# Sharing the residual update of three norms between two engines, and moving four other pieces of work

## The chip, the cores and the metric

One core of a Trainium2 chip runs the whole program. The time is the device time of one execution in microseconds (us), lower is better. Profiled executions add a span (first to last instruction) and a trace.

## What is computed

Two transformer layers over 512 tokens of width 1024 (with 256 context tokens beside them in layer 0), then a third block with windowed attention and a mixture of experts. Cut to what matters here:

```python
for i in range(2):                      # layer i; the context rows are dropped after layer 0
    hx = rmsnorm(x, g_pre_mix[i]) * (1 + sc1) + sh1        # "premix" norm
    px = hx @ w_in[i]
    attn = attention(rope(q), rope(k), v)                  # 8 heads, keys of x and of ctx
    four = fft2(px[..., F0:H0]).real @ w_fourier[i]
    hy   = x0 * longconv(x1 * v, filter)                   # hyena
    x = x + ga1 * rmsnorm(concat(attn, four, hy) @ w_out[i], g_post_mix[i])   # "postmix", then "preffn"
    x = x + ga2 * rmsnorm(conv_ffn(rmsnorm(x)...), g_post_ffn[i])             # "postffn"
# third block: attention, router, experts; each token goes to the two best of 16 experts
```

The modulation vectors (`sc1`, `sh1`, `ga1`, ...) are a product of the condition with a large matrix, whose slabs are streamed in between the other weights.

## The kernel before, in words

Activations lie transposed: 8 blocks of 128 channels (`x[:, k, :]`) by 768 tokens (layer 0, `T`) or 512 (`TX`). Each product is done in three passes of split operands (a high part and a remainder), so every weight slab of 128x1024 is loaded by a DMA of SyncE, copied to `whi` by ScalarE and its remainder `wlo` is made by GpSimd (L585). A ring of three slots holds the raw slabs; SyncE loads the next one when a slot is free (L506 to L512). The order on each engine is the order of the code; semaphores tie the engines.

**Norm to norm.** After the output product, `post_norm` (L1966) gates the 8 blocks of `y` on VectorE (two instructions a block at 768 tokens, one at 512). GpSimd adds block k to `x` when it is gated (L591). ScalarE squares it (`norm_stats`, L1407) into one of two buffers, TensorE sums the squares (L718), and when the eighth is summed the inverse root mean square goes back over ScalarE, VectorE and TensorE to the scaling of the next norm. This happens four times: layer 0 postmix (768 tokens), layer 0 postffn (768), layer 1 postmix (512) and layer 1 postffn, which the change leaves as it is.

**Fourier and first attention steps.** TensorE makes `fab` tiles (L909), waits for all of them and for all five rotated heads (`k_roped`), and runs for f = 0, 1 the second Fourier product (L941, segment 0 of 512 tokens and in layer 0 segment 1 of 256), each followed by the scores of two attention steps (L928, `scores(0)` and `scores(2)`). Then comes the output product (L954), then six transposes of the values (L961), ScalarE's `values_hi` and VectorE's `values_lo`, and only then the first transposes of probabilities (L971). From there attention is a loop of equal steps.

**Hyena.** `hy_pair(p)` multiplies two slabs of the modulation matrix (L755, eight instructions); they lie in the ring's slots, and the loads of the next pair are issued when a pair is used. `mod_turn` (L763) transposes the result of two pairs. Pairs 0 and 1 and the turn stand before the first transform product, pair 2 behind the second product of f = 0, pair 3 inside f = 1, pair 4 inside f = 3. The filter product (L1033) waits for the table `hd5`, the input product is L1045, the inverse L1066.

**Experts.** GpSimd issues four scatters of token rows to `slot_rows` (L614), waits until they have landed, issues seven loads `xs` (L617, L619), and only then makes the remainders `mlo` of 21 of the 168 expert slabs (L623), VectorE those of the others (L2568). TensorE's product of the second expert (`gate_up(1)`, slab 1) needs the first of them, its third expert (`gate_up(2)`) begins with `turn_block(1, 0)`, which waits for all the loads `xs` (L1313). Raw expert slabs stand in 8 slots; SyncE loads slab n when the remainder of slab n - 8 is made, so slab 13 waits for GpSimd's first remainder (slab 5).

Of the kernel before, what the change touches and what calls it, by code (L numbers as in the profile page):

```python
# [29 lines left out]
P = 128  # L30
D = 1024
KT = D // P
# [116 lines left out]
def program(nc, dram, out):  # L149
# [187 lines left out]

    def sum_nth(key):

        return 0 if key == norms[0] else 1 + post_nth(key)  # L340
# [231 lines left out]
    def _(pool):  # L572
# [38 lines left out]
        pool.wait_ge(sem("slots_clear"), 16)  # L611
        pool.wait_ge(sem("routed"), 5)
        for tt in range(TX // P):
            pool.indirect_dma_start(slots_d, bass.IndirectOffsetOnAxis(slot_i[:, tt:tt + 1], 0), xrow[:, tt, :], None)\  # L614
                .then_inc(sem("rows_placed"), 16)
        pool.wait_ge(sem("rows_placed"), 16 * (TX // P))
# [3 lines left out]
        for u, j in M_POOL:  # L620
            n = M_AT[(u, j)]
            pool.wait_ge(ring_hi, n + 1)
            pool.tensor_tensor(mlo2[:, n % MS, :], mraw2[:, n % MR, :], mhi2[:, n % MS, :].bitcast(F32),  # L623
                               ALU.subtract).then_inc(pool_lo, 1)
# [8 lines left out]
    def _(pe):  # L633
# [174 lines left out]
        for L in range(DEPTH):  # L808
# [122 lines left out]

            pe.wait_ge(sem("fab_ready"), T // P * L + ntt)
            pe.wait_ge(sem("k_roped"), 5 * L + 5)
            for f in range(2):
# [24 lines left out]
            pe.wait_ge(sem("qk_lo"), 5 * L + 5)  # L959
            for tt in range(6):  # L960
                m = pe.transpose(ps[:, 4 + tt // 4, (tt % 4) * P:(tt % 4) * P + P], pxq[:, PXV, tt * P:tt * P + P],  # L961
                                 ident[:, :])
            m.then_inc(sem("vt_done"), 1)
# [51 lines left out]
            hy_pair(1)  # L1015
            mod_turn(HY_G[L], 3)
            two = len(hsegs[L]) == 2
            for s, c0, nt_ in hsegs[L]:
# [9 lines left out]
                for f in range(nt_):  # L1028
# [20 lines left out]
                    if s == 0 and f == 0:  # L1049
                        hy_pair(2)  # L1050
# [330 lines left out]
    def _(act):  # L1381
# [19 lines left out]
        def norm_stats(key, src, width, ready=None, before=0):  # L1401
            for k in range(KT):
                if ready is not None:
                    act.wait_ge(ready, before + k + 1)
                if k >= 2:
                    act.wait_ge(sem("sq_used"), (KT + 1) * sq_nth(key) + k - 1)
                act.activation(nsq[:, k % 2, 0:width], src[:, k, 0:width], ACT.Square)\  # L1407
                   .then_inc(sem("sq_ready"), 1)
# [73 lines left out]
        for L in range(DEPTH):  # L1482
# [3 lines left out]
            else:  # L1486
                norm_stats((L, "premix"), x, T, sem("x_ready"), KT * post_nth((L - 1, "postffn")))
# [7 lines left out]
            if L == 0:  # L1495
                act.dma_start(fl2[:, :, :, :], dram["four256"]).then_inc(sem("ftab_in", L), 16)
                act.dma_start(slots_d, dram["slot_rows"]).then_inc(sem("slots_clear"), 16)
# [94 lines left out]

            def scaled_act(i):
# [6 lines left out]
            for f in range(2):  # L1600
# [18 lines left out]

            def values_hi():  # L1620
                act.wait_ge(sem("vt_done"), L + 1)
                for g in range(2):
                    h = slice(64 * g, 64 * g + 64)
                    m = act.activation(vth[:, g, :, h], psf[:, 2048:2048 + 768].rearrange("p (t n) -> p t n", t=6)[:, :, h],
                                       ACT.Copy)
                m.then_inc(sem("pt_hi"), 1)
# [12 lines left out]
            values_hi()  # L1639
# [32 lines left out]
            for s, c0, nt_ in hsegs[L]:  # L1672
                w = nt_ * P
                K = (L, s)
                for f in range(nt_):
# [6 lines left out]
                    if s == 0 and f == 1:  # L1682
# [26 lines left out]
            norm_stats((L, "preffn"), x, W, sem("x_ready"), KT * post_nth((L, "postmix")))  # L1709
# [45 lines left out]
        unnormed((2, "premix"), TX, sem("x_ready"), KT * post_nth((1, "postffn")),  # L1755
# [164 lines left out]
    def _(dve):  # L1920
# [45 lines left out]
        def post_norm(key, L, gate, width, low=None):  # L1966

            inverse_rms(key, width)
            for k in range(KT if low is None else KT + 3):
# [5 lines left out]
                if low is not None and k >= 3:  # L1975
                    low(k - 3)
            dve.drain()
# [50 lines left out]
        for L in range(DEPTH):  # L2028
# [116 lines left out]
            for c in range(2):  # L2145
                bv = V0 + V_HYB + c
                dve.tensor_scalar(hub[:, c, 0:W], pxh[:, 2 + c, 0:W], vec[:, bv:bv + 1], None, ALU.mult)
            if L == 0:
# [28 lines left out]
            minimum(2)  # L2177
            minimum(3)
# [12 lines left out]
            def values_lo():  # L2191
                dve.wait_ge(sem("pt_hi"), (HALVES0 + 1) * L + 1)
                for g in range(2):
                    h, other = slice(64 * g, 64 * g + 64), slice(64 - 64 * g, 128 - 64 * g)
                    dve.memset(vth[:, g, :, other].bitcast(F32), 0.0)
                    dve.memset(vtl[:, g, :, other].bitcast(F32), 0.0)
                    m = dve.tensor_tensor(vtl[:, g, :, h], psf[:, 2048:2048 + 768].rearrange("p (t n) -> p t n", t=6)[:, :, h],
                                          vth[:, g, :, h].bitcast(F32), ALU.subtract)
                m.then_inc(sem("pt_lo"), 1)

# [10 lines left out]
            values_lo()  # L2211
# [219 lines left out]
        dve.wait_ge(sem("router_in"), 64)  # L2431
# [391 lines left out]
```

## Time and profile before

| | us |
|---|---|
| median of 3 runs (2543.62 to 2550.24) | 2543.91 |
| profiled execution | 2553.14 |
| its span | 2551.3 |
| TensorE busy in it | 2343.3 (92%) |
| VectorE, ScalarE, GpSimd busy | 1285.1, 1099.0, 652.1 |
| mean granted TensorE clock (of 2.4 GHz) | 0.954 |

PE is TensorE (PEld its weight loads), DVE VectorE, ACT ScalarE, POOL GpSimd, SP SyncE; a letter q behind a name is its queue or sequencer. In a timeline row the columns are start, duration, engine, line, operation, what is written <- what is read, shape and count; in brackets stands how long the engine had been idle and who released it. A row of several instructions gives their busy time together.

### The profile page before, as it was taken

The numbers are of one execution on the slowest core, as the hardware profiler recorded it, in microseconds if no ns is written. First come the engines' busy times: TensorE is split into PE (matmuls) and PEld (weight loads), VectorE is DVE, ScalarE is ACT, GpSimd is POOL, SyncE is SP. The second block draws the span as 40 slices with busy tenths as digits, with TensorE's granted clock in tenths as the row PEclk, the third lists the DMA queues.
The fourth block names the chain that finished last, engine by engine and source line by source line (L and its number), as shares of the span: only waits on it lengthen the run. The fifth ranks groups of instructions, "written<-read, shape, count | busy, mean of one in ns | idle before, by whom it ended". The sixth has DMA issues, their size and how long they took to land.

```text
span 2551.3 us, 32346 instructions
## 1 busy us (share of the span) xinstructions
PE 2343.3 (92%) x12442; PEld 1869.8 (73%) x12442; DVE 1285.1 (50%) x2040; ACT 1099.0 (43%) x1687; POOL 652.1 (26%) x295
## 2 busy tenths in 40 slices
PE   4998979979999999988989888999999999979997
PEld 2875856858888788866657566888876877767776
DVE  3565942153431344235667214534524269449998
ACT  3423840353332333225357035434423268447776
POOL 1220000242222222342300034444444410222223
PEclk8999999979999999988989998999999999989999
DMA  6421032113222232112400441233332322249997
GB/s 240 174 96 34 1 118 97 58 36 114 92 66 67 83 118 73 58 50 95 140 1 32 151 148 59 96 95 98 99 97 69 98 69 59 111 152 366 346 350 262
DMA packets 81466, 291.27 MB, mean 114 GB/s; under 512 B 10761, under 2 KB 13226, under 8 KB 80364
## 3 DMA queue, kind: packets, MB, share of 16 engines
q1 hardware_dynamic: 74192, 257.68, 30.0%
q10 hardware_dynamic: 4252, 20.58, 2.2%
q0 software_dynamic: 2880, 11.06, 1.1%
q8 instruction: 96, 1.57, 0.2%
q14 instruction: 46, 0.38, 0.0%
HBM read 283.50 MB, written 9.48 MB: 115 GB/s over the span
## 4 chain that ended last, share of the span: by engine, by line
PE 77%; DVE 11%; ACT 3%; DMA 2%; POOL 2%; issue 2%; DVEq 1%; SPq 0%; POOLq 0%; ACTq 0%
PE ps L647 37%; PE ps L694 12%; DVE mlo L2568 5%; PE ps L670 4%; PE ps L985 3%; PE ps L971 2%; PE ps L1347 2%; PE ps L755 2%; PE ps L1207 2%; PE ps L928 2%; POOL x L591 1%; PE ps L941 1%; PE ps L1045 1%; PE ps L1066 1%; DMA wraw<-in_w_all 1%
## 5 line engine op out<-in xcount | busy, mean ns | idle before, releaser
L585 POOL TENSOR_TENSOR wlo<-wraw,whi 128x1024 fp32r<-128x1024 f32 x208 | 502.1, 2415 | 1386.1 <-ACT whi L1388 738.9
L647 PE MATMUL ps<-hhi,whi 128*128 128x512 f32 x1624 | 591.8, 364 | 3.0 <-DVE hlo L2265 2.0
L647 PE MATMUL ps<-hlo,whi 128*128 128x512 f32 x1624 | 583.3, 359 | 0.0
L647 PE MATMUL ps<-hhi,wlo 128*128 128x512 f32 x1624 | 580.7, 358 | 0.0
L647 PEld LDWEIGHTS ps<-hhi,whi 128*128 128x128 f32 x1624 | 306.2, 189 | 83.3 <-issue 31.2
L647 PEld LDWEIGHTS ps<-hhi,wlo 128*128 128x128 f32 x1624 | 305.3, 188 | 47.9
L647 PEld LDWEIGHTS ps<-hlo,whi 128*128 128x128 f32 x1624 | 306.2, 189 | 45.3 <-issue 1.0
L1982 DVE SCALAR_TENSOR_TENSOR up<-ps,cconv,up 128x511 f32<-128x511 f32 (+1 forms) x132 | 83.1, 658 | 294.9 <-ACT up L1725 292.3
L2568 DVE TENSOR_TENSOR mlo<-mraw,mhi 128x1024 fp32r<-128x1024 f32 x147 | 203.8, 1415 | 9.7 <-ACT mhi L1851 9.2
L1395 ACT ACTIVATE whi<-wraw 128x1024 fp32r<-128x1024 f32 x132 | 138.9, 1052 | 152.6 <-PE ps L694 120.3
L1725 ACT ACTIVATE up<-ps,cconv 128x768 f32<-128x768 f32 (+1 forms) x88 | 77.8, 884 | 257.7 <-PE ps L647 257.2
L694 PE MATMUL ps<-alo,whi 128*128 128x512 f32 (+1 forms) x528 | 188.0, 356 | 0.0
L694 PE MATMUL ps<-ahi,whi 128*128 128x512 f32 (+1 forms) x528 | 187.4, 355 | 0.0
L694 PE MATMUL ps<-ahi,wlo 128*128 128x512 f32 (+1 forms) x528 | 186.6, 353 | 0.0
L1851 ACT ACTIVATE mhi<-mraw 128x1024 fp32r<-128x1024 f32 x168 | 167.4, 1050 | 5.7 <-DMA mraw<-in_w_moe 5.3
L2314 DVE TENSOR_TENSOR y<-y,ps 128x768 f32<-128x768 f32 (+1 forms) x32 | 26.2, 820 | 227.6 <-PE ps L694 227.6
L1388 ACT ACTIVATE whi<-wraw 128x1024 fp32r<-128x1024 f32 x76 | 80.2, 1057 | 111.5 <-PE ps L647 86.8
L694 PEld LDWEIGHTS ps<-ahi,whi 128*128 128x128 f32 x528 | 99.6, 189 | 15.0
L694 PEld LDWEIGHTS ps<-ahi,wlo 128*128 128x128 f32 x528 | 99.2, 188 | 14.8
L694 PEld LDWEIGHTS ps<-alo,whi 128*128 128x128 f32 x528 | 99.5, 188 | 13.8
L623 POOL TENSOR_TENSOR mlo<-mraw,mhi 128x1024 fp32r<-128x1024 f32 x21 | 62.8, 2990 | 177.0 <-ACT mhi L1851 177.0
L670 PE MATMUL ps<-hhi,whi 128*128 128x512 f32 (+1 forms) x168 | 68.3, 406 | 31.8 <-DVE hlo L1960 23.1
(360 smaller groups left out, 4210.7 us busy)
## 6 DMA issues: line engine op xcount, KB each, us to landing
wraw<-in_w_all SPq DMA_DIRECT2D x288, 512.0 KB, 3.6
mraw<-in_w_moe SPq DMA_DIRECT2D x168, 512.0 KB, 5.7
mraw_b<-in_w_mod SPq DMA_DIRECT2D x10, 512.0 KB, 15.4
fl<-in_four ACTq DMA_DIRECT2D x2, 2048.0 KB, 8.2
hi<-in_hyi ACTq DMA_DIRECT2D x2, 2048.0 KB, 8.7
slot_rows<-in_slot_rows ACTq DMA_DIRECT2D x1, 3612.0 KB, 20.9
xs<-slot_rows POOLq DMA_DIRECT2D x7, 516.0 KB, 6.9
mraw_a<-in_w_mod SPq DMA_DIRECT2D x6, 512.0 KB, 10.5
```

Of the source, the lines that this page charges most:

```text
L585: pool.tensor_tensor(wlo[:, slot, :], wraw[:, AT_W[n] % RING, :], whi[:, slot, :].bitcast(F32), ALU.subtract).then_inc(lo_split, 1)
L623: pool.tensor_tensor(mlo2[:, n % MS, :], mraw2[:, n % MR, :], mhi2[:, n % MS, :].bitcast(F32), ALU.subtract).then_inc(pool_lo, 1)
L647: m = pe.matmul(ps[:, bank + b, 0:w], a, r[:, c0:c0 + w], start=k == 0 and q == 0, stop=k == KT - 1 and q == 2)
L670: m = pe.matmul(ps[:, bank + b, 0:w], a, r[:, c0:c0 + w], start=k == 0 and q == 0, stop=k == KT - 1 and q == 2)
L694: m = pe.matmul(ps[:, bank + b, 0:w], a, r[:, c0:c0 + w], start=k == 0 and z == 0, stop=k == PAIRS - 1 and z == 2)
L985: m = pe.matmul(ps[:, 6 + ht % 2, c0:c0 + HALF], u[:, g, kts[c], :], w[:, unit % 2, c, g * HALF:g * HALF + HALF], start=g == 0 and c == 0 ...
L1388: act.activation(whi[:, n % RING, :], wraw[:, AT_W[n] % RING, :], ACT.Copy).then_inc(hi_split, 1)
L1395: act.activation(whi[:, n % RING, :], wraw[:, AT_W[n] % RING, :], ACT.Copy).then_inc(hi_split, 1)
L1725: act.activation(up[:, p % 2, z, 0:W], psf[:, b * 512:b * 512 + W], ACT.Identity, bias=cconv[:, s, 3:4], scale=cconv[:, s, 1:2]).then_inc( ...
L1851: act.activation(mhi2[:, m % MS, :], mraw2[:, n % MR, :], ACT.Copy).then_inc(ring_hi, 1)
L1982: dve.scalar_tensor_tensor(dst[:, c0 + 1:c0 + w], ps[:, bank + b, 0:w - 1], w0, dst[:, c0 + 1:c0 + w], ALU.mult, ALU.add)
L2568: dve.tensor_tensor(mlo2[:, m % MS, :], mraw2[:, n % MR, :], mhi2[:, m % MS, :].bitcast(F32), ALU.subtract).then_inc(ring_lo, 1)
```

## The change

Five edits. (1) In three of the four post norms GpSimd adds blocks 0 to 4 and VectorE blocks 5 to 7, with a semaphore of its own; ScalarE squares in the order 0, 1, 2, 3, 5, 4, 6, 7. (2) The transposes of the values stand behind the first Fourier segment and use PSUM banks 0 and 1, the wait for the rotated heads stands behind that segment, `values_hi` and `values_lo` follow at once; `scores(0)` stands behind segment 0 of f = 1 and `scores(2)` behind the output product, and ScalarE's and VectorE's parts follow that order. (3) In hyena one pair stands between the two products of each of the four f, and the turns behind the second product of f = 0 and 2. (4) GpSimd makes its first `mlo` before it waits for the scatters. (5) The clearing of `slot_rows` counts on `router_in`.

```diff
+    def pool_adds(key):
+        return KT if key == (DEPTH - 1, "postffn") else 5
+    def added(key, k):
+        n = post_nth(key)
+        return (sem("x_ready"), 5 * n + k + 1) if k < pool_adds(key) else (sem("x_late"), 3 * n + k - 4)
...
-                for k in range(KT):
+                for k in range(pool_adds(key)):
                     pool.wait_ge(sem("y_gated"), KT * post_nth(key) + k + 1)
...
                 if key[1] == "postmix":
+                    pool.wait_ge(sem("x_late"), 3 * post_nth(key) + 3)
                     pool.drain()
...
+        mlo(*list(M_POOL)[0])
         pool.wait_ge(sem("rows_placed"), 16 * (TX // P))
...
-        for u, j in M_POOL:
...
+        for u, j in list(M_POOL)[1:]:
+            mlo(u, j)
...
             pe.wait_ge(sem("fab_ready"), T // P * L + ntt)
-            pe.wait_ge(sem("k_roped"), 5 * L + 5)
...
-                if f == 0:
-                    pe.wait_ge(sem("qk_lo"), 5 * L + 5)
-                scores(2 * f)
+                    if s == 0 and f == 0:
+                        pe.wait_ge(sem("k_roped"), 5 * L + 5)
+                        turned_values()
+                    if s == 0 and f == 1:
+                        pe.wait_ge(sem("qk_lo"), 5 * L + 5)
+                        pe.wait_ge(sem("pt_lo"), (HALVES0 + 1) * L + 1)
+                        scores(0)
...
+            scores(2)
...
-            hy_pair(1)
-            mod_turn(HY_G[L], 3)
...
-                    if s == 0 and f == 1:
-                        hy_pair(3)
-                    if s == 0 and f == 2:
-                        mod_turn(HY_G[L] + 1, 3)
-                    if s == 0 and f == 3:
-                        hy_pair(4)
+                    if s == 0:
+                        hy_pair(1 + f)
...
-                    if s == 0 and f == 0:
-                        hy_pair(2)
+                    if s == 0 and f in (0, 2):
+                        mod_turn(HY_G[L] + f // 2, 3)
...
+            for k, b in enumerate((0, 1, 2, 3, 5, 4, 6, 7)):
+                act.wait_ge(*added(post, b))
...
-                exponentials(2 * f)
-                exponentials(2 * f + 1)
-                if f == 0:
-                    scaled_act(1)
+                    if s == 0 and f == 0:
+                        values_hi()
+            exponentials(0)
+            exponentials(1)
+            scaled_act(1)
...
+            exponentials(2)
+            exponentials(3)
...
-                    if s == 0 and f == 1:
+                    if s == 0 and f == 2:
                         rows(HY_G[L] + 1, 3)
...
+            def add(k):
+                dve.tensor_tensor(x[:, k, 0:width], x[:, k, 0:width], y[:, k, 0:width], ALU.add)\
+                   .then_inc(sem("x_late"), 1)
...
+                if pool_adds(key) < KT and k >= 6:
+                    dve.drain()
+                    add(k - 1)
+            if pool_adds(key) < KT:
+                add(KT - 1)
```

## Rows read from the trace of the kernel before

**Rows 1.** Page, part 4: shares of the chain that ended last.

```profile
PE 77%; DVE 11%; ACT 3%; DMA 2%; POOL 2%; issue 2%; DVEq 1%; SPq 0%; POOLq 0%; ACTq 0%
```

**Rows 2.** Timeline of layer 0's postmix to preffn norm, 768 tokens.

```profile
512.65 8.49 DVE L1972 SCALAR_TENSOR_TENSOR y<-y,mv,ps 128x512 f32<-128x512 f32 x16 [2.32 <-PE ps L747]
513.87 14.22 POOL L591 TENSOR_TENSOR x<-x,y 128x768 f32<-128x768 f32 x8 [1.34 <-DVE y L1972]
...
528.12 0.84 ACT L1407 ACTIVATE nsq<-x 128x768 f32<-128x768 f32 x1 [0.93 <-POOL x L591]
...
529.02 1.08 PE L718 MATMUL ps<-nsq,ones 128*32 128x256 f32 x8 [0.69 <-ACT nsq L1407]
```

**Rows 3.** Timeline of layer 1's postmix to preffn norm, 512 tokens.

```profile
1525.49 9.86 POOL L591 TENSOR_TENSOR x<-x,y 128x512 f32<-128x512 f32 x8
...
1536.07 0.66 PE L718 MATMUL ps<-nsq,ones 128*32 128x128 f32 x8 [0.57 <-ACT nsq L1407]
```

**Rows 4.** Line 2302: operation, count, duration in ns (min/median/max), starts, forms.

```profile
L2302 DVE TENSOR_TENSOR alo<-sil,ahi x44: 691/825/961, 569.5 to 1853.0; 128x768 fp32r<-128x768 f32 x22, 128x512 fp32r<-128x512 f32 x22
```

**Rows 5.** Timelines of VectorE and of GpSimd, early in the experts.

```profile
2305.65 3.40 DVE L2568 TENSOR_TENSOR mlo<-mraw,mhi 128x1024 fp32r<-128x1024 f32 x2 [0.76 <-ACT mhi L1851]
...
2303.96 2.88 POOL L623 TENSOR_TENSOR mlo<-mraw,mhi 128x1024 fp32r<-128x1024 f32 x1 [12.01 <-ACT mhi L1851]
```

**Rows 6.** Timeline of layer 0, Fourier to the first attention loop step.

```profile
214.29 0.60 ACT L1570 ACTIVATE fab<-ps 128x512 f32<-128x512 f32 x1 [0.30 <-PE ps L909]
...
216.23 10.53 PE L941 MATMUL ps<-fl,fab 128*128 128x512 f32 x24 [1.98 <-DVE pxq L2131]
...
227.94 8.86 PE L941 MATMUL ps<-fl,fab 128*128 128x512 f32 x24
...
237.97 5.43 PE L954 MATMUL ps<-fy,wfo 128*128 128x512 f32 x16
...
240.84 0.86 ACT L1617 ACTIVATE hhi<-ps 128x512 fp32r<-128x512 f32 x2
...
249.75 0.49 ACT L1635 ACTIVATE pth<-ps 128x384 fp32r<-128x384 f32 x1 [3.62 <-PE ps L971]
```

**Rows 7.** Timeline of the same stretch in layer 1.

```profile
1282.55 10.02 PE L941 MATMUL ps<-fl,fab 128*128 128x512 f32 x16 [4.48 <-DVE pxq L2131]
...
1293.74 7.13 PE L941 MATMUL ps<-fl,fab 128*128 128x512 f32 x16
...
1312.58 0.49 ACT L1635 ACTIVATE pth<-ps 128x384 fp32r<-128x384 f32 x1 [3.62 <-PE ps L971]
```

**Rows 8.** One window: busy time by engine, then PEclk, DMA share, GB/s.

```profile
218.00:220.00 2.00, 2.00 (x3) 0.69 (x3) 2.00 (x4) 0.63 (x2) 0.00 (x0) 0.50 0.00 0
```

**Rows 9.** DMA issues (KB, us to landing), then timeline, of hyena in layer 0.

```profile
hd<-in_hyf ACTq DMA_DIRECT2D x1, 512.0 KB, 4.7
...
367.07 5.19 PE L1033 MATMUL ps<-hpm,hd 128*128 128x256 f32 x16
...
382.60 1.06 PE L755 MATMUL ps<-wraw,cs 128*32 128x512 f32 x8 [2.24 <-DMA wraw<-in_w_all]
383.59 5.41 PE L1045 MATMUL ps<-hut,hd 128*128 128x256 f32 x16
...
392.73 3.62 PE L1045 MATMUL ps<-hut,hd 128*128 128x256 f32 x16
```

**Rows 10.** Hyena in layer 1: chain (start, duration, what), then timeline.

```profile
1397.43 9.62 DMA hd<-in_hyf
...
1423.25 1.07 PE L755 MATMUL ps<-wraw,cs 128*32 128x512 f32 x8 [2.27 <-DMA wraw<-in_w_all]
```

**Rows 11.** Experts: a wait; GpSimd's DMA queue (packets, MB, share), 2283-2296, 2276-2280.

```profile
PE ps L1347 <- POOL mlo L623: 4.7, 1, 4.7
...
q0 software_dynamic: 990, 3.65, 74.0%
...
q0 software_dynamic: 204, 0.78, 47.2%
```

More of the change, by code:

```diff
@@ L609, in _ @@
                     m.then_inc(sem("osum_ready"), 1)
-        pool.wait_ge(sem("slots_clear"), 16)
+        pool.wait_ge(sem("router_in"), 16)
         pool.wait_ge(sem("routed"), 5)
@@ L615, in _, with mlo @@
                 .then_inc(sem("rows_placed"), 16)
+        def mlo(u, j):
+            n = M_AT[(u, j)]
+            pool.wait_ge(ring_hi, n + 1)
+            pool.tensor_tensor(mlo2[:, n % MS, :], mraw2[:, n % MR, :], mhi2[:, n % MS, :].bitcast(F32),
+                               ALU.subtract).then_inc(pool_lo, 1)
+        mlo(*list(M_POOL)[0])
         pool.wait_ge(sem("rows_placed"), 16 * (TX // P))
@@ L619, in _ @@
             pool.dma_start(xs[:, b, :], slots_d[b * P:b * P + P, :]).then_inc(sem("blocks_in"), 16)
-        for u, j in M_POOL:
[L621 to L624, printed above, removed]
+        for u, j in list(M_POOL)[1:]:
+            mlo(u, j)
         for b in range(BLOCKS):
@@ L930, in scores, with turned_values @@
                 m.then_inc(sem("s_ready"), 2)
+            def turned_values():
+                for tt in range(6):
+                    m = pe.transpose(ps[:, tt // 4, (tt % 4) * P:(tt % 4) * P + P], pxq[:, PXV, tt * P:tt * P + P],
+                                     ident[:, :])
+                m.then_inc(sem("vt_done"), 1)
             pe.wait_ge(sem("fab_ready"), T // P * L + ntt)
-            pe.wait_ge(sem("k_roped"), 5 * L + 5)
             for f in range(2):
@@ L955, in _ @@
                     m.then_inc(sem("fst3"), 1)
+            scores(2)
             pe.wait_ge(sem("k_roped"), 5 * L + 5)
             pe.wait_ge(sem("four_out"), 4 * L + 2 * len(fseg))
[L959 to L963, printed above, removed]
             def transposed(i):
@@ L1399, in rms, with norm_stats @@
                .then_inc(sem("std_ready"), 1)
[L1401 to L1404, printed above, removed]
+        def norm_stats(key, width, post):
+            for k, b in enumerate((0, 1, 2, 3, 5, 4, 6, 7)):
+                act.wait_ge(*added(post, b))
                 if k >= 2:
                     act.wait_ge(sem("sq_used"), (KT + 1) * sq_nth(key) + k - 1)
-                act.activation(nsq[:, k % 2, 0:width], src[:, k, 0:width], ACT.Square)\
+                act.activation(nsq[:, k % 2, 0:width], x[:, b, 0:width], ACT.Square)\
                    .then_inc(sem("sq_ready"), 1)
@@ L1486, in _ @@
             else:
-                norm_stats((L, "premix"), x, T, sem("x_ready"), KT * post_nth((L - 1, "postffn")))
+                norm_stats((L, "premix"), T, (L - 1, "postffn"))
             norm_apply((L, "premix"), T, *mods(L, 0, 0), late_rows if L == 0 else None)
@@ L1496, in _ @@
                 act.dma_start(fl2[:, :, :, :], dram["four256"]).then_inc(sem("ftab_in", L), 16)
-                act.dma_start(slots_d, dram["slot_rows"]).then_inc(sem("slots_clear"), 16)
+                act.dma_start(slots_d, dram["slot_rows"]).then_inc(sem("router_in"), 16)
             def head_std(j):
@@ L1591, in exponentials, with values_hi @@
                    .then_inc(sem("exp_done"), 1)
+            def values_hi():
+                act.wait_ge(sem("vt_done"), L + 1)
+                act.wait_ge(sem("qk_lo"), 5 * L + 5)
+                for g in range(2):
+                    h = slice(64 * g, 64 * g + 64)
+                    m = act.activation(vth[:, g, :, h], psf[:, 0:768].rearrange("p (t n) -> p t n", t=6)[:, :, h],
+                                       ACT.Copy)
+                m.then_inc(sem("pt_hi"), 1)
             def scaled_act(i):
@@ L1618, in _ @@
                                    ACT.Copy).then_inc(sem("four_hi"), 1)
[L1620 to L1626, printed above, removed]
+            exponentials(2)
+            exponentials(3)
             def transposed_hi(i):
@@ L1708, in _ @@
             split(S0 + IN_T + OUT_T - 1 + RING)
-            norm_stats((L, "preffn"), x, W, sem("x_ready"), KT * post_nth((L, "postmix")))
+            norm_stats((L, "preffn"), W, (L, "postmix"))
             norm_apply((L, "preffn"), W, *mods(L, 2, 3))
@@ L1752, in _ @@
             summed_rms((L, "postffn"), W)
-        unnormed((2, "premix"), TX, sem("x_ready"), KT * post_nth((1, "postffn")),
+        unnormed((2, "premix"), TX, sem("x_ready"), 5 * post_nth((1, "postffn")),
                  lambda k: vec[:, V2_MIX + k:V2_MIX + k + 1], 3)
@@ L2147, in _, with values_lo @@
                 dve.tensor_scalar(hub[:, c, 0:W], pxh[:, 2 + c, 0:W], vec[:, bv:bv + 1], None, ALU.mult)
+            def values_lo():
+                dve.wait_ge(sem("pt_hi"), (HALVES0 + 1) * L + 1)
+                for g in range(2):
+                    h, other = slice(64 * g, 64 * g + 64), slice(64 - 64 * g, 128 - 64 * g)
+                    dve.memset(vth[:, g, :, other].bitcast(F32), 0.0)
+                    dve.memset(vtl[:, g, :, other].bitcast(F32), 0.0)
+                    m = dve.tensor_tensor(vtl[:, g, :, h], psf[:, 0:768].rearrange("p (t n) -> p t n", t=6)[:, :, h],
+                                          vth[:, g, :, h].bitcast(F32), ALU.subtract)
+                m.then_inc(sem("pt_lo"), 1)
+            values_lo()
             if L == 0:
@@ L2176, in _ @@
             scaled(1)
-            minimum(2)
-            minimum(3)
             fseg = hsegs[L]
@@ L2190, in _ @@
                        .then_inc(sem("four_out"), 1)
[L2191 to L2199, printed above, removed]
+            minimum(2)
+            minimum(3)
             def transposed_lo(i):
@@ L2209, in transposed_lo @@
                        .then_inc(sem("pt_lo"), 1)
-            values_lo()
             for i in range(2, max(shares) + 1, 2):
@@ L2430, in _ @@
                                      xt(tt), ALU.mult, ALU.add).then_inc(sem("xrow_ready"), 1)
-        dve.wait_ge(sem("router_in"), 64)
+        dve.wait_ge(sem("router_in"), 80)
         dve.tensor_tensor(wgr[:, :, :], wgr[:, :, :],
```

1 line of the change is left out of this document (removed).

## Prediction

> **What bounds the kernel now.** I first read the page's chain of work that ended last: three quarters of it are TensorE's [rows 1], so an edit pays only where TensorE stands still or runs at the lower clock. I then walked the chain in order of time, looked for the places where it leaves TensorE, and opened the timelines of those that the edits touch. There are five kinds. At a norm the chain is GpSimd's eight additions, back to back, with the squares following one by one [rows 2, 3]. In the Fourier stage TensorE waits for rotated heads that its next product doesn't read, and later for the values [rows 6, 7]. In hyena it waits for modulation slabs and for the table [rows 9, 10]. In the experts it waits for GpSimd's first remainder [rows 11]. And behind such holes the granted clock falls from 1.00 to 0.50 (from 2.4 to 1.2 GHz): TensorE stood idle 1.98 us before 216.23, and 218 to 220 us was granted 0.50 [rows 6, 8].
>
> **Norms, 768 tokens (two).** GpSimd's additions take 14.22 / 8 = 1.78 us each [rows 2]; five of them end at 513.87 + 8.89 = 522.76. VectorE gates a block in 8.49 / 8 = 1.06, so block 6 is gated at 520.1. VectorE's addition is priced by a two-input operation of the same shapes, 0.96 us [rows 4]. If the engines did not disturb each other the last block would be there at 524.2. But such a pair in collision stands in [rows 5]: GpSimd's remainder ran from 2303.96 to 2306.84, and VectorE's two, started at 2305.65, took 3.40 where two cost 2.4 (the first ended only some 1.1 us behind GpSimd's). So I let the eight additions follow one another: 5 x 1.78 + 3 x 0.96 = 11.8, to 525.6. The square (0.84) and its sum (1.08) and 0.1 for the hand-overs end at 527.6, where the last sum now ends at 529.02 + 1.08 = 530.10 [rows 2]: 2.5 us. Without collision TensorE's own pace of 1.08 for a sum sets the end, near 527.1: 3.0. If VectorE always lost to GpSimd, its block 5 would come at 523.7 and the last at 526.7: 1.5. The Trainium skill (SBUF — State Buffer, "Who interferes with whom") speaks against the split: a VectorE operation with two SBUF inputs and a GpSimd operation that reads SBUF want the same pair of ports, and whichever starts first holds it for its whole instruction while the other blocks. The trace agrees in [rows 5]; by this rule a norm gives the 2.5 us of the serial order, or 1.5 if GpSimd leaves no gap, and not 3.0.
>
> **Norm, 512 tokens (one).** Five additions of 1.23 and three of 0.69 [rows 3, 4] are 8.2 us, to 1533.7; square and sum end at 1535.1 instead of 1536.73: 1.5 (0.6 to 2.2). What follows is paced as before: the first FFN product and layer 1's in-projection start when the normed blocks come. The new wait on GpSimd, for VectorE's additions before it clears `y`, holds up only the clearing and the next remainder, needed 15 us and more later. Together **6.5 us**, bounds 3.6 and 8.2.
>
> **Fourier and attention, layer 0.** The wait for the rotated heads moves behind the first segment, so TensorE starts when the last `fab` is copied, 214.29 + 0.60 = 214.9, not at 216.23. The short gap should not cost the clock; now it does: 10.53 us for what costs 8.86 in the second round [rows 6]. At the higher clock a 512-token segment costs 6.9 (7.13 with its tail [rows 7]) and the 256-token one 1.75. The new order is 6.9, transposes 0.7, 1.75, 6.9, scores 1.2 (the hole between 226.8 and 227.94), 1.75: 234.1. The last `fy` copy holds TensorE until 234.6, the output product takes 5.2, scores(2) starts at 239.8 and ends at 241.0. From the end of scores(2) to the point where ScalarE has done the two exponentials pass 240.84 - 237.97 = 2.9 us [rows 6], so it takes the first transposed probabilities at 244.0; now it does at 249.75. The values' copies (five to six us now between 243.4 and 248.84) lie beside the Fourier products: ScalarE has 6.9 us there with two short copies, and VectorE comes from its last `hub` at 223.5 to values_lo, done near 226.2, before scores(0) needs it at 231.1. If that cover failed each us would be paid. **5.5 us**; 3.4 if the low clock stays as it is, 5.8 at most. Moved exponentials 2 and 3 stand ahead of ScalarE's first transposed copy; that is counted, it is what is late next.
>
> **Layer 1.** TensorE's hole of 4.48 us [rows 7] shrinks to the copy of 0.6, and the first round costs 6.9 instead of 10.02. From 1278.8: 6.9, 0.7, 6.9, 1.2, output product 8 x 0.43 = 3.4, to 1297.9. Here ScalarE is busy with exponentials 0, 1 and a scaling until 1298.6, then copies two outputs (0.6 each), VectorE's remainders and minimum follow to 1301.5, and two exponentials end at 1303.5; the row of before is 1312.58. **9.1 us**; 6.2 if the clock falls as now.
>
> **Hyena, layer 0.** Pair 1 and its turn no longer stand before the first filter product. That product then waits only for the table, issued at 357.9 and landed 4.7 us later [rows 9]: 362.7 instead of 367.1, 4.4 us won. The pair (1.04) and the turn (0.44) return inside: 1.5 lost. The stall of pair 3, 2.24, goes: between two pairs there are now at least 7 us of products, and a pair's slab lands 3.6 to 5.7 us behind its issue. With it goes the slow product behind it, 5.41 against 3.62: 1.8. Sum 6.9; the two tables of 2 and 1 MB are now issued close to the slabs, so I take **6.5**, bounds 3.5 (a new low clock and one new stall) and 8. **Layer 1**: the 2 MB table landed in 9.62 us beside four slabs [rows 10], two of which are now issued later; that is 1 MB at some 0.4 MB a us less, but up to 1.7 us only, since the last was barely begun: 1.7 won, 1.5 lost, the stall of 2.27 gone: **2.3**, bounds 0.8 and 3.
>
> **Experts.** GpSimd's first remainder now comes at 2279.4 to 2282, so TensorE's wait of 4.7 [rows 11] goes and slab 13 is issued 7 us earlier. But TensorE's next unit begins with a block of `xs`. These loads, 3.65 MB on GpSimd's queue, had the engines nearly alone in 2283 to 2296 (74% of them [rows 11]); now five or more slabs are issued beside them, and when both queues were at work before, GpSimd's got 47% [rows 11]. At half of 0.4 MB a us they land near 2301, and TensorE, which took its first block of them at 2299.5, waits 8 us and starts at the low clock. From there on VectorE is nearly always busy, so that what the first block loses stays lost. Bounds: 4.7 won if the loads keep their priority, 4 lost. The 47% speaks for the lower half, so I take **1 us lost**. The counter on `router_in` (both loads long landed) costs nothing; if it weren't landed GpSimd's scatter would wait, which 35 us and more of distance exclude.
>
> **Sum.** 6.5 + 5.5 + 9.1 + 6.5 + 2.3 - 1.0 = 28.9 us. The profiled execution's span of 2551.3 (2553.14 in all) becomes 2522.4; the median of the runs lies 9 us under the profiled one, and I subtract the same from it: 2543.91 - 28.9 = **2515.0**.
>
> **Rivals.**
> *The experts keep the whole gain:* `xs` lands in time, +4.7 instead of -1; together with undisturbed norms (+1.7) it is 2507.5. For it: GpSimd's queue moved all and SyncE's nothing until 2293 in the old order, though four slabs were issued at 2289.7. Against it: 47% when both were running.
> *The clock falls anyway* in both Fourier starts and in hyena: 2.1 + 2.9 + 3 less, 2523. For it: holes of 0.6 us for the last `fab` copy and of 4 us for the table stay ahead of the two stages, and an idle time of 1.98 us was enough for 0.50 in 218 to 220 us [rows 6, 8]. Against it: in Fourier the hole shrinks to a third or less.
> *Slower:* the denser order keeps TensorE at 1.2 GHz through Fourier and hyena of both layers. The fast-clock work there is some 130 us, so half of it would already cost 65 us, 2580. It decides once over 36 us more than now run at the lower clock. Each of the falls in [rows 6, 7] costs 1.7 to 3 us, so it would need some twenty such, where the change takes holes away.
> *It doesn't do what it says:* VectorE's additions queue behind GpSimd's so that the last block comes no earlier; the norms give 0 to 3 in place of 6.5, 2519.
>
> **How the numbers follow.** The forecast, within 5 us: 0.50. All expert and norm gains: 0.17. Clock falls: 0.18. Norms without gain: 0.10. Slower: 0.02, and 0.03 for a mixture that leaves under 7.6 us of gain. The range from 2504 to 2527 takes in the first four with the bounds of the hyena and Fourier terms. About 0.3% (7.6 us) is what a measurement here tells from no change: faster 0.95, within 0.03, slower 0.02.
>
> **What would show it.** Last sum of squares 2.5 us earlier relative to the gating (1.5 at 512); additions stretched on one of the two engines. No TensorE idle over 1 us ahead of L941, and no transposes of values behind L954. No wait of L755 for a slab between the f of hyena. In the experts no wait of L1347 for L623, but one of the transposes of `xs` for their loads. The prediction is wrong if the first attention step isn't 5 and 9 us earlier, counted from the in-projection's end, for these two terms are half of the sum.

## The result and the profile after

The changed kernel takes **2530.34 us** (median of 6 runs, 2526.65 to 2533.26); the kernel before on the same chips 2547.07 (6 runs, 2538.74 to 2551.5). The ratio is 0.994, 95% interval 0.9925 to 0.9956: 15 us faster, 11 to 19. Forecast were 28.9 us and 2515.0, with a range from 2504 to 2527, and 2530.34 lies outside it. A second measurement (e8 below) gave 0.9939 again. The direction was right; half of the gain didn't come.

The profiled execution of the changed kernel has a span of 2528.4 us, against 2551.3. The first lines of part 1 and of part 4 of its page show that TensorE is busy 14 us less with as many instructions and holds more of the chain, GpSimd less [rows 1]:

```profile
PE 2329.0 (92%) x12442; PEld 1862.8 (74%) x12442; DVE 1295.6 (51%) x2049; ACT 1097.1 (43%) x1687; POOL 646.4 (26%) x286
...
PE 80%; DVE 10%; ACT 3%; DMA 2%; issue 2%; POOL 1%; DVEq 1%; SPq 0%; ACTq 0%
```

**Norms.** Timeline of layer 0's postmix norm (the last of VectorE's additions also by itself, from a narrower window), then of layer 1's, the answers to [rows 2, 3]:

```profile
499.18 7.44 DVE L1992 SCALAR_TENSOR_TENSOR y<-y,mv,ps 128x512 f32<-128x512 f32 x14 [2.56 <-PE ps L761]
500.40 9.63 POOL L600 TENSOR_TENSOR x<-x,y 128x768 f32<-128x768 f32 x5 [1.57 <-DVE y L1992]
...
506.71 1.64 DVE L1986 TENSOR_TENSOR x<-x,y 128x768 f32<-128x768 f32 x1
...
509.50 2.22 DVE L1986 TENSOR_TENSOR x<-x,y 128x768 f32<-128x768 f32 x2
...
510.78 0.94 DVE L1986 TENSOR_TENSOR x<-x,y 128x768 f32<-128x768 f32 x1
...
513.07 1.08 PE L732 MATMUL ps<-nsq,ones 128*32 128x256 f32 x8 [0.17 <-ACT nsq L1419]
...
1500.76 7.08 POOL L600 TENSOR_TENSOR x<-x,y 128x512 f32<-128x512 f32 x5
...
1510.02 0.66 PE L732 MATMUL ps<-nsq,ones 128*32 128x128 f32 x8 [0.29 <-ACT nsq L1419]
```

From GpSimd's first addition to the end of the last sum pass 514.15 - 500.40 = 13.75 us; before, 530.10 - 513.87 = 16.23. VectorE's first addition started at 506.71 beside the fourth of GpSimd, which ran until 507.54, and took 1.64. GpSimd's fifth started at 507.49 and took 2.55, where the other four took 1.81 to 1.82. VectorE's last one ran alone and took 0.94, against the 0.96 of the prediction.

**Fourier.** Timeline, layer 0 and layer 1: the first second-stage product and the first transposed probabilities [rows 6, 7]:

```profile
214.28 7.13 PE L960 MATMUL ps<-fl,fab 128*128 128x512 f32 x16 [0.69 <-ACT fab L1582]
...
243.77 0.87 ACT L1651 ACTIVATE pth<-ps 128x384 fp32r<-128x384 f32 x2
...
1260.66 7.13 PE L960 MATMUL ps<-fl,fab 128*128 128x512 f32 x16 [0.69 <-ACT fab L1582]
...
1285.12 0.87 ACT L1651 ACTIVATE pth<-ps 128x384 fp32r<-128x384 f32 x2
```

TensorE is idle 0.69 us instead of 1.98 and 4.48, and the segment costs 7.13. The granted clock was 1.00 (2.4 GHz) from 214 to 222 us, where before it was 0.50 from 218 to 220 [rows 8].

**Hyena, layer 1.** Timeline of TensorE and, from the chain, the table's load (start, duration) [rows 10]; the last line is the first filter product in the kernel before:

```profile
1370.12 10.76 DMA hd<-in_hyf
...
1380.93 6.61 PE L1050 MATMUL ps<-hpm,hd 128*128 128x256 f32 x16 [9.15 <-DMA hd<-in_hyf]
...
1397.65 1.06 PE L769 MATMUL ps<-wraw,cs 128*32 128x512 f32 x8 [1.57 <-DMA wraw<-in_w_all]
...
1440.73 1.30 PE L769 MATMUL ps<-wraw,cs 128*32 128x512 f32 x8 [4.01 <-DMA wraw<-in_w_all]
...
1407.10 5.78 PE L1033 MATMUL ps<-hpm,hd 128*128 128x256 f32 x16 [2.19 <-DMA hd<-in_hyf]
```

SyncE's queue moved less between the table's issue and its landing (1.05 MB, before 1.42), and the table still lands later: 10.76 us after its issue, not 9.62. TensorE stands idle for 9.15 us of it, and its product behind the wait takes 6.61 us, not 5.78. The granted clock was 0.50 from 1381 to 1385, the first 4 us of that product; in the kernel before it was 0.59 from 1408 to 1412.

**Experts.** GpSimd's first remainder and loads, TensorE's longest wait (waits: us, times, longest), and the DMA queues (packets, MB, share; q1 carries SyncE's slabs, q0 GpSimd's loads) in the 13 us from the loads' issue on, then in 2255 to 2259, then in 2261 to 2275 [rows 11]:

```profile
2251.35 2.50 POOL L629 TENSOR_TENSOR mlo<-mraw,mhi 128x1024 fp32r<-128x1024 f32 x1 [4.85 <-ACT mhi L1866]
...
2255.23 0.59 POOL L634 DMA_DIRECT2D xs<-slot_rows  x1 [1.38 <-DMA slot_rows<-xrow,slot_i]
...
PE ps L1330 <- issue: 14.1, 1, 14.1
...
q1 hardware_dynamic: 703, 2.56, 55.2%
q0 software_dynamic: 540, 2.02, 41.4%
...
q1 hardware_dynamic: 283, 1.02, 84.8%
q0 software_dynamic: 5, 0.02, 6.7%
...
q0 software_dynamic: 801, 2.94, 51.8%
q1 hardware_dynamic: 774, 2.84, 50.3%
```

The wait of 4.7 us for the remainder is gone, and one of 14.1 us for `xs` stands in its place. In the first 4 us the slabs had the engines nearly alone (1.02 MB against 0.02); after that the two queues moved equal parts.

### The profile page after: what moved, and what is told of

Read it like the earlier page. It is cut to its first block, busy times and chain, and to the rows that moved or that the text cites. A ratio compares the mean times of both kernels' runs of the same rounds, so it can differ in the third digit from the quotient of the medians.

```text
span 2528.4 us, 32354 instructions
## 1 busy us (share of the span) xinstructions
PE 2329.0 (92%) x12442; PEld 1862.8 (74%) x12442; DVE 1295.6 (51%) x2049; ACT 1097.1 (43%) x1687; POOL 646.4 (26%) x286
## 3 DMA queue, kind: packets, MB, share of 16 engines
q8 instruction: 96, 1.57, 0.3%
## 4 chain that ended last, share of the span: by engine, by line
PE 80%; DVE 10%; ACT 3%; DMA 2%; issue 2%; POOL 1%; DVEq 1%; SPq 0%; ACTq 0%
PE ps L661 38%; PE ps L708 12%; PE ps L684 5%; DVE mlo L2593 4%; PE ps L1004 3%; PE ps L1360 2%; PE ps L990 2%; PE ps L769 2%; PE ps L1220 2%; PE ps L1378 1%; PE ps L942 1%; PE ps L1079 1%; PE ps L960 1%; POOL x L600 1%; PE ps L1050 1%
## 5 line engine op out<-in xcount | busy, mean ns | idle before, releaser
L684 PE MATMUL ps<-hhi,whi 128*128 128x512 f32 (+1 forms) x168 | 68.3, 407 | 32.1 <-DVE hlo L1975 22.5
## 6 DMA issues: line engine op xcount, KB each, us to landing
mraw_a<-in_w_mod SPq DMA_DIRECT2D x6, 512.0 KB, 10.8
```

The costliest lines, as they stand in the source:

```text
L684: m = pe.matmul(ps[:, bank + b, 0:w], a, r[:, c0:c0 + w], start=k == 0 and q == 0, stop=k == KT - 1 and q == 2)
```

## Stage by stage

Every experiment left a profile, 14 with the two kernels. Their runs scatter by 3 to 8 us to either side of the median, so I read each term as the length of a stage between two events that the edits don't touch, and took the mean over all profiles that have the edit and over all that haven't: Fourier from the first square of the heads (`qsq`) to the first transposed probabilities (`pth`); hyena from there to the post norm's first addition; a norm from that addition to the first `sil` of the FFN (ScalarE's) or the next `qsq`; experts from the first scatter to VectorE's first addition to `xs`.

| stage | forecast gain | without the edit (profiles) | with it (profiles) | measured gain |
|---|---|---|---|---|
| Fourier, layer 0 | 5.5 | 174.6 (5) | 170.2 (9) | 4.4 |
| Fourier, layer 1 | 9.1 | 131.9 (5) | 124.9 (9) | 7.0 |
| hyena, layer 0 | 6.5 | 263.2 (5) | 258.4 (9) | 4.8 |
| hyena, layer 1 | 2.3 | 213.2 (5) | 216.5 (6) | -3.3 |
| three norms | 6.5 | 131.5 (5) | 123.2 (9) | 8.3 |
| experts | -1.0 | 66.3 (6) | 73.2 (3) | -6.9 |
| sum | 28.9 | | | 14.3 |

The sum agrees with the measured 15, and no other stretch differs by more than its scatter. Two of the means hide something. In Fourier, layer 0, seven of the nine profiles with the edit lie at 169.6 and two (e2, e7) at 172.4; in those two 6.8 us of the stage ran at the lower clock (granted clock 0.50), ahead of the Fourier products, and in the seven none did. And hyena, layer 1, scatters: 211.0 to 215.2 without the edit, 214.6 to 219.1 with it.

## The experiments

Each time is a median with its range; the kernel before ran beside it.

**The kernel before, again.**

> The kernel before, run as if it were a changed one, for two things: the spread of the comparison, and a second profile. If the first profiled execution (2553.14 us) was typical, the span comes out near 2551 again. If it was a long one of its kind (the medians of before and after lie 16.7 us apart, the two spans 22.9), the span is nearer to 2545, and the missing 6 us can be located by setting the two traces side by side. Ratio 1.000 within 0.002.

Measured: 2545.86 us (2537.78 to 2550.48, 11 runs) against 2546.64; ratio 0.9994 (0.9981 to 1.0007). Its span is 2545.3, 6.0 us shorter than that of the profile on which the prediction rests. Side by side the excess lies in scattered places, among them the Fourier start of layer 1. Timeline of this second profile there (compare 10.02 after 4.48 in [rows 7]):

```profile
1279.76 8.80 PE L941 MATMUL ps<-fl,fab 128*128 128x512 f32 x16 [2.78 <-DVE pxq L2131]
...
1289.74 7.13 PE L941 MATMUL ps<-fl,fab 128*128 128x512 f32 x16
```

**Only the early remainder.**

```diff
+        mlo(*list(M_POOL)[0])
         pool.wait_ge(sem("rows_placed"), 16 * (TX // P))
```

> Before, with edits 4 and 5 alone: GpSimd's first remainder ahead of the wait for the scatters. Theory A (the loads xs are shared out against slabs issued earlier, and TensorE's third expert waits for the last of them): TensorE waits about 14 us once instead of 4.7, and the time is 5 to 7 us longer than before. Theory B (the experts' loss in the changed kernel has to do with the other edits, which let everything arrive in another phase): 1 us longer to 5 us shorter.

Measured: 2556.96 (2549.23 to 2562.98) against 2546.64; ratio 1.0047 (1.0033 to 1.0061), 12 us slower. TensorE's wait for `xs` is 12.81 us, the experts' stage 73.1 against 66.3. That is theory A, and theory B, 1 us longer at most, is excluded; but the time grew by more than the 5 to 7 us said. The stage explains 6.8 of 10 to 12 us; where the rest is I can't tell, since the profiled execution (2549.23) was the shortest of the five.

**All but the early remainder.**

> The changed kernel without edit 4 (GpSimd waits for the scatters first, as before). Theory A: TensorE's one wait is 4.7 us again, and it is 5 to 7 us faster than the changed kernel, about 2524. Theory B: within 1 us of the changed kernel.

Measured: 2524.82 (2520.67 to 2531.36); ratio 0.9911 (0.9896 to 0.9926), 22 us faster than before and 5.5 faster than the changed kernel, as theory A has it. TensorE's wait for the remainder is back (3.6 us, said were 4.7), the stage is 65.8.

**A counter of its own for block 1.**

```diff
-            pe.wait_ge(sem("blocks_in"), 16 * (BLOCKS - 1))
+            if b == 1:
+                pe.wait_ge(sem("first_block_in"), 32)
+            else:
+                pe.wait_ge(sem("blocks_in"), 16 * (BLOCKS - 2))
```

> The changed kernel, where TensorE's transposes of block 1 of xs wait for the loads of blocks 0 and 1 alone (counted on the counter of block 0), those of blocks 2 to 6 for the other five loads. Theory A: what the third expert waits for is the last of six loads sharing the DMA engines with slabs; the first two land within some 4 us of their issue, so the wait of 14 us goes nearly whole, slabs take part of it back since the engines are full, and it is 6 to 12 us faster than the changed kernel. Rival: the slabs are what is short, not xs; then TensorE waits for a remainder in place of xs, and the time is within 2 us of the changed kernel.

The loads of blocks 0 and 1 count on `first_block_in` in this kernel; VectorE's wait on it counts both too.

Measured: 2522.42 (2514.07 to 2527.43); ratio 0.9901 (0.9883 to 0.9918), 8 us faster than the changed kernel. Its waits of TensorE early in the experts:

```profile
PE ps L1342 <- DVE eact L2624: 2.1, 1, 2.1
PE ps L1334 <- issue: 1.3, 1, 1.3
```

The last of the loads still lands 19.9 us after its issue, but nobody waits for it: the wait of 14 us was for blocks 2 to 6, which are used 36 us later and beyond.

**Hyena alone.**

> Before, with edit 3 alone. Theory C (read from the changed kernel's trace: in layer 1 the 2 MB table lands no earlier though two slabs are issued later, so the pair and the turn that used to run inside that wait now cost time of their own): layer 0 gains about 5 us from the first transposed probabilities to the post norm's first addition, layer 1 loses about 4 us in the same stretch; together within 3 us of before. Theory D (the layer-1 loss comes from the Fourier edit's new phase or from chance): layer 1 gains 0 to 2.5 us and the time is 5 to 9 us shorter.

Measured: 2541.32 (2537.9 to 2550.75) against 2546.72; ratio 0.9981 (0.9968 to 0.9994), 2 to 8 us faster. By the time alone C and D aren't told apart; the medians, 5.4 us apart, are nearer to D. By the stages layer 0 gained 3.0 us in this profile, and layer 1, at 215.1, lost 1.8, which is within the scatter of the profiles without the edit. What speaks for C is the table: it landed 10.7 us after its issue (9.1 to 9.6 in all five profiles with the old order, 10.2 to 10.8 in the six with the new one). It takes e7 below to decide.

**Fourier alone.**

> Before, with edit 2 alone. By the prediction 5.5 + 9.1 = 14.6 us shorter. By the changed kernel's trace, counted from the first squares of the heads to the first transposed probabilities, 5.3 us in layer 0 and 6.8 us in layer 1, so 12 us. The two differ in layer 1 alone: how much of the hole of 4.48 us in front of the first product was there to be won.

Measured: 2534.62 (2529.88 to 2542.86); ratio 0.9954 (0.9936 to 0.9972), 12 us faster, as the second reading said. The interval, 7 to 16 us, doesn't exclude the 14.6 forecast; the two stages, 5.0 and 6.0 us shorter in this profile than the means without the edit, do not reach it.

**Norms alone.**

> Before, with edits 1 and 5 alone. Serial theory (GpSimd's and VectorE's additions exclude each other): last sum of squares 2.5 us earlier at 768 tokens, 1.3 to 1.5 us at 512, 6.5 us in all. The changed kernel's trace counted from the first addition to the first product behind the norm gave 3.2, 4.0 and 2.2, 9.4 us in all; if those 2.9 us more belong to edit 1, the time is 9 us shorter, if to chance or another edit, 6.5.

Measured: 2539.48 (2529.39 to 2544.31); ratio 0.9961 (0.9947 to 0.9975), 7.2 us by the medians, 10 by the ratio. In its profile the last sum ends 13.75, 13.75 and 9.92 us after the first addition, against 16.23, 16.22 and 11.24: 6.3 us, the serial sum, and the three stages gain 6.6 in all. In the changed kernel the second norm has 13.32 and its stage 40.7 instead of 42.0: there the higher clock was back within the norm. Windows of the changed kernel's second norm, 9.3 and 12.3 us after its first addition on, and then here, 12.3 us after it on (busy time of each engine, then PEclk, DMA share, GB/s):

```profile
1128.00:1131.00 3.00, 2.43 (x24) 0.44 (x16) 2.03 (x2) 2.18 (x3) 0.34 (x1) 0.53 0.00 0
1131.00:1134.00 3.00, 2.20 (x24) 1.57 (x20) 0.00 (x0) 0.70 (x2) 0.00 (x0) 1.00 0.03 5
```

```profile
1144.00:1147.00 3.00, 2.33 (x17) 1.28 (x14) 0.00 (x0) 0.67 (x2) 0.00 (x0) 0.50 0.00 0
```

All profiles with the edit agree. In the two where the three stages hold as much time at the lower clock as without the edit (83.5 and 83.7 us in e6 and e10, against 84.1 in the mean) they gain 6.6 and 6.3 us; where it is 68.3 and 68.8 us (e3, e11), they gain 10.5 and 9.2. So the split itself gives some 6.5 us, and in some profiles the earlier return of the clock adds up to 4. The run times here fit 6.5 and 9 alike.

**Pair 1 back in layer 1**, on top of the counter for block 1.

```diff
+            if L == 1:
+                hy_pair(1)
+                mod_turn(HY_G[L], 3)
...
-                    if s == 0:
+                    if s == 0 and (L == 0 or f > 0):
                         hy_pair(1 + f)
```

> The kernel of e3_block1_counter with one more edit: in layer 1 pair 1 and its turn stand before the first filter product again. Theory C: the pair and the turn hide in the wait for the 2 MB table again, and layer 1's hyena stage gives back 2 to 4 us: about 2519.5. Theory D: no change. Rival: the table lands earlier as before but the next pair's slabs collide with it again, stall of 2 us back: within 1 us.

Measured: 2516.95 (2513.62 to 2520.35); ratio 0.9875 (0.9861 to 0.989). Layer 1's hyena stage is 213.1 again (213.1 to 213.2 in all three kernels that have this) instead of 216.5. Its timeline and the table's load:

```profile
1377.32 1.94 PE L770 MATMUL ps<-wraw,cs 128*32 128x512 f32 x8 [1.53 <-DMA wraw<-in_w_all]
...
1384.65 5.11 PE L1054 MATMUL ps<-hpm,hd 128*128 128x256 f32 x16 [3.57 <-DMA hd<-in_hyf]
...
1374.14 10.46 DMA hd<-in_hyf
```

The table lands no sooner; the pair and the turn lie inside its wait again, and the slabs of the next pair don't stall it. Theory C. The run times put the step from e3 at 5.5 us. The stage is 6.0 us shorter than in e3's profile, which has the longest of the six, and 3.4 shorter than their mean.

**The changed kernel, again.**

> The changed kernel once more, beside the three others of this call and for a second profile of it. Stages as in its first profile to within the scatter of the two profiles of before (each stage within some 2 us, the experts' hole before the third expert 13 to 15 us); ratio to before 0.994 within 0.002.

Measured: 2527.49 (2526.19 to 2536.7) against 2544.24; ratio 0.9939 (0.992 to 0.9959). The wait for `xs` is 13.34 us.

**Slabs held back** until `xs` has landed, in the changed kernel.

```diff
+            if n == MR + 5:
+                sp.wait_ge(sem("blocks_in"), 16 * (BLOCKS - 1))
```

> The changed kernel, but SyncE issues slab 13 and all behind it only when the seven loads xs have landed, so that nothing is shared with them except the slabs issued before. Theory A (sharing with slabs delays xs): the last of xs lands some 10 to 13 us after its issue instead of 19.5, TensorE's wait for xs shrinks from 14 us to 2 to 6, and a wait for the remainders of the held slabs of some 2 to 5 us appears behind it; net 2 to 8 us faster than the changed kernel. Rival E (GpSimd's queue is slow because its descriptors are written late while VectorE holds the ports, whatever SyncE does): xs still lands 17 to 20 us after its issue, TensorE still waits 14 us, and the held slabs make it 3 us or more slower.

Measured: 2527.13 (2520.64 to 2532.15); ratio 0.9926 (0.9906 to 0.9946), 0 to 3 us faster than the changed kernel beside it, which the run times can't tell from no change. First come TensorE's waits, then the time from each load's own issue to its landing (min, median, max; for all on tile `xs`) here and in the changed kernel, then the queues in 2255 to 2268, from the loads' issue on:

```profile
PE ps L1332 <- issue: 3.1, 1, 3.1
PE ps L1340 <- DVE eact L2622: 2.6, 1, 2.6
```

```profile
DMA to landing us min/median/max: 3.3/4.4/9.1
```

```profile
DMA to landing us min/median/max: 3.3/6.0/19.5
```

```profile
q0 software_dynamic: 1008, 3.70, 73.9%
q1 hardware_dynamic: 107, 0.37, 7.3%
```

With the slabs held back the slowest of the same loads lands 9.1 us after its issue, with them beside it 19.5: sharing is the cause, not GpSimd's queue, so rival E is excluded. The stage is 67.9, 5.3 us shorter; the run times show less of that than the profile.

**The kernel of e7 without the early remainder.**

> The kernel of e7_pair1_back_in_layer1 without edit 4. It asks what the early remainder is worth once its side effect is gone. By the prediction's sum the wait of 4.7 us comes back, at the lower clock behind it: 4 to 6 us slower than e7. Rival: with xs landing sooner the experts lose the same time elsewhere (remainders on VectorE), 0 to 2 us slower.

Measured: 2518.31 (2514.63 to 2523.99); ratio 0.9891 (0.9873 to 0.9909). TensorE waits 4.2 us for the remainder, and the experts' stage is 67.0 against 62.5 in e7. Run times put the difference at 1 to 4 us, with intervals that overlap; the stage puts it at 4.5. So by the stage the early remainder is worth nearly its 4.7 us, but only where the third expert doesn't wait for all of `xs`.

**Later loads of blocks 2 to 6.**

```diff
+            if i == 1:
+                for b in range(2, BLOCKS):
+                    pool.dma_start(xs[:, b, :], slots_d[b * P:b * P + P, :]).then_inc(sem("blocks_in"), 16)
```

> The kernel of e7_pair1_back_in_layer1, where GpSimd issues the loads of blocks 2 to 6 behind its third remainder instead of before its second: some 12 us later, when they are still 25 us ahead of their first use. If the DMA engines' shared time is what still delays slabs there (waits of 1 to 2 us for VectorE's results behind late slabs), it is 1 to 3 us faster than e7; if these waits have another cause, within 1 us; if the loads then collide with slabs of the fourth expert, 1 to 3 us slower.

Measured: **2513.78** (2509.33 to 2516.21); ratio 0.9878 (0.9859 to 0.9897) against 0.9875 for e7: no difference from e7 that this can tell (stage 62.3 against 62.5). It and e7 beat both kernels, by 30 us against before and by about 14 against the changed one.

## Why the prediction was right in direction and wrong in size

**Where 14.6 us went.** The forecast was a sum of six terms, 28.9 us, and the stages gained 14.3. The experts are 5.9 us short and hyena of layer 1 is 5.6; the two Fourier terms are 1.1 and 2.1 short and hyena of layer 0 is 1.7; the norms gained 1.8 more. (The sums held small roundings, 5.75 booked as 5.5 and 2.5 as 2.3.) So two steps of the prediction failed above all: in the experts "at half of 0.4 MB a us they land near 2301", booked as 1 us lost, and in hyena of layer 1 "1.7 won" from a table that was to land sooner. Part of the rest is the profile that the gains were read from.

**Experts: -6.9 instead of -1.** The mechanism was named: the loads `xs` share the engines with slabs issued earlier, and the third expert waits for the last of them. e1, e2, e3 and e9 bear it out. Its size was wrong. I took the landing at near 2301 on the time scale of before, some 18 us after the issue. The loads were issued at 2255.23, where before they were at 2283.35, so on that scale the measured end of the wait, 2278.0, lies at 2306.1: five us later than I had it. Half of the engines was the right rate once both queues moved (2.94 MB against 2.84 in 14 us); what I left out is the start. In the first 4 us after the issue the slabs had the engines, and the loads moved 0.02 MB of 3.65. Nor had I gone on to count what the landing that I did name costs: TensorE waiting 8 us in place of 4.7 was put down as 1 lost, with -4 for the bound. The Trainium skill (DMA: Bandwidth & Descriptors, "Queues, rings and completion order") says that each engine goes round the queue rows it has work for, packet by packet; the trace agrees from 2261 on, with 51.8% to 50.3%. The loads' old 74% [rows 11] was mostly an empty neighbour: the next slabs were issued 6.3 us behind the loads, and e9, where they are held back, shows 73.9% again. The rival "the experts keep the whole gain" read it as a priority. What it had for it is in the trace (from 2289.7 to 2292.2 only GpSimd's queue moved, 0.97 MB, though slabs were issued), but from 2293 to 2295 the shares were 53% to 47%. It is refuted by the wait of 14.1 us; its +4.7 exists, but behind a counter that the change doesn't have (e10 against e7).

**Hyena, layer 1: -3.3 instead of +2.3.** The failed step is "that is 1 MB at some 0.4 MB a us less", booked as 1.7 won. There was no 1 MB beside the table to take away: the two later slabs were issued 5.7 us behind it, and SyncE's queue moved 1.42 MB until the table had landed, against 1.05 MB in the changed kernel. And the table took 10.2 to 10.8 us instead of 9.1 to 9.6 with less beside it. As the table lands no sooner, everything that is taken out of the wait is paid. Between the two profiles the stage differs by 2.7 us: the table comes 1.15 later, the pair and the turn cost 1.04 and 0.44, the product behind the wait 0.83 more at the lower clock, and the stall of 2.27 shrank by only 0.7 to 1.57. e7 shows it from the other side.

Why the table lands 1 us later is not shown by an experiment, but the traces hold a candidate: a 16 KB packet on the queue of instruction loads (q8). This is it beside the table in the changed kernel, in 1375 to 1377 (packets, MB, share):

```profile
q8 instruction: 1, 0.02, 2.8%
```

It falls 5.4 to 7.3 us after the table's issue in all nine profiles where the table took 10.2 to 10.8 us (e7, e10 and e11 among them), and 9.4 to 10.6 us after it, behind the table's last packet, in all five where it took less. In the nine the table's last data packet ends 0.8 us behind the one before it, in the five 0.1 to 0.4. No run moves this packet alone, so it stays a coincidence of 14 in 14.

**The profile that the gains were read from.** From the start of the Fourier products to the first transposed probabilities I had worked out 29.1 us for layer 0 (214.9 to 244.0) and 24.7 for layer 1 (1278.8 to 1303.5); measured are 29.49 and 24.46, in all nine profiles with the edit to within 0.05. But the 30.03 us that layer 1's stretch took in [rows 7] is the longest of five profiles with the old order (30.03, 28.85, 28.81, 27.12, 27.11). The whole stage was 133.4 there and 131.9 in the mean: 1.4 of the 2.1 us that this term is short were never there to win. Over the six stages that profile is 3.7 us longer than the mean of those without the edit. "The median of the runs lies 9 us under the profiled one, and I subtract the same from it" holds if the edits leave alone whatever made that execution long. Here part of that excess was low clock behind the very holes that the edits close. The median it was subtracted from was itself 3.2 us low: 2543.91 of three runs, 2547.07 of six.

**Fourier, layer 0: 4.4 instead of 5.5.** In seven of nine profiles the gain is 5.3, as forecast; the mean is lower for the two with low clock ahead of the products.

**Hyena, layer 0: 4.8 instead of 6.5.** The first product came 4.5 us earlier in the mean, as said (4.4). The stalls behind it didn't vanish, they shrank: 0.88 us before a pair in place of 2.24.

**Norms: 8.3 instead of 6.5.** The serial sum held to 0.2 us (13.7 worked out to the last sum, 13.75 measured; 6.3 over the three norms in e6). The Trainium skill's rule of the shared ports (SBUF — State Buffer, "Who interferes with whom") agrees: VectorE's first addition ended 0.82 us behind GpSimd's fourth, GpSimd's fifth 1.68 us behind VectorE's. The rest is the clock, which I had left out in favour of the change.

**Rivals and signs.** "The clock falls anyway" didn't occur at the Fourier starts: 7.13 both times. In hyena of layer 1 it did: 27.9 to 31.4 us of the stage ran at the lower clock, against 21.8 to 27.5. But it was as much in the kernels with pair 1 back (28.5 to 31.7), whose stage is 213.1 again, so it doesn't explain the loss. "It doesn't do what it says" is excluded by e6, "slower" by the result. Of the signs named beforehand, the hole before the Fourier products, the sums of squares and the wait for `xs` came as said. The waits of the modulation products for a slab stayed (0.88 and 1.57), and the first attention step came 5.3 us earlier in most profiles and 7.0 in the mean, not 5 and 9. Missing was a rival in which several terms are overstated together, because all were read from one execution.

## What to carry to other kernels

When a transfer's issue moves earlier, ask which transfer shares the engines with it then and who waits for the last byte of that one; a counter that bundles the urgent load with five others turns sharing into a stall. Count the start too: bytes already queued ahead can cost more than the halved rate suggests. Work taken out of a wait for a transfer is paid in full unless the transfer itself comes earlier, and that has to be shown, not assumed from the bytes beside it. Before a sum is made against one profiled execution, see how far its span lies from the median: an execution that is long by 6 us shows holes and low clock that a typical one doesn't have, and edits that close holes seem to win them.

## What the runs showed of the hardware

Two queues with work at once divided the DMA engines' time evenly (51.8% and 50.3% in 2261 to 2275), but a load issued behind queued slabs moved only 0.02 MB in its first 4 us. The slowest of seven loads of 3.65 MB together landed 19.5 us after its own issue instead of 11.5, and 9.1 with the slabs held back. VectorE's and GpSimd's additions of two SBUF operands ran one after the other: 1.64 and 2.55 us where they met, 0.94 and 1.8 where they didn't. A 2 MB table took 9.1 to 9.6 us in the order of before, 10.2 to 10.8 in the new one, and 10.5 with the old slab order again (e7): the slabs beside it don't explain it, and what goes with it in all 14 profiles is a 16 KB instruction packet inside the table's transfer. Executions of one kernel scatter by 3 to 8 us to either side of the median. The total time at the lower clock differs by 5.5 us (237.5 and 232.0) between the two profiles of the kernel before; it is 215.2 in that of the changed one.
